# A two-block transformer kernel: the order of high and low weight products inside a half unit

## The chip, the cores and the metric

The kernel runs on one core of one Trainium2 chip. The metric is the device time of one execution, in microseconds. Before the change it is 2764.68 us, the median of three runs (2763.32 to 2768.03). Smaller is better.

## The reference

The program computes two transformer blocks on 256 tokens of width 2048, all in float32. What matters here is that nearly all of its work is products of activations with large weights:

```
first block:   h = rmsnorm(x);  proj = h @ w_in   (RG-LRU, rope attention with sinks, gates)
               x = x + rmsnorm(mix @ w_out)
               u = square(relu(rmsnorm(x) @ w_mlp_up));  x = x + rmsnorm(u @ w_mlp_down)
second block:  h = rmsnorm_2(x);  proj = h @ w_in   (dilated, block-sparse and compressed attention)
               x = x + concat(o_a, o_b, o_c) @ w_out
               a, g = split(conv3(rmsnorm_2(x) @ w_up));  x = x + (silu(g) * a) @ w_down
out = rmsnorm_2(x)
```

## The kernel before, in words

TensorE multiplies in fp32r, a format that keeps fewer bits than float32. To keep float32 accuracy, every operand is split in two: a high part, which is the value rounded to fp32r, and a low part, which is the value minus its high part. A product is then high weight times high activation, plus high weight times low activation, plus low weight times high activation.

**Tiling.** Activations are held with features on the partitions: a tile such as `h2` is 128 partitions x 16 chunks x (high, low) x 256 tokens. One output tile of 128 features x 256 tokens needs 16 chunks of 128 input features. The weights for it, 128 x 16 x 128 values, are a *unit* (1 MB; FD units have 11 chunks). The table `STREAM` lists 25 stages with their numbers of units, in the order in which they are used (X, RG, Q, Y, V, G, MR, MA, O, UP0, DN0, and so on to FD1). Each unit is worked off in two *half units* of 8 chunks (6 and 5 in FD).

**The weights' way.** SyncE loads a unit into `w_raw` (two buffers). ScalarE (line 1278, `half_hi`) copies a half unit to `w_hi`, rounding it, and raises `hi_ready`. VectorE (line 1972, `half_lo`) subtracts `w_hi` from `w_raw` into `w_lo` and raises `lo_ready`; only then may SyncE load the next unit into that `w_raw` buffer. There are four places for half units in `w2`. ScalarE overwrites a place when `half_done` shows that TensorE has finished the half unit that lay there.

**The products.** `half_unit` (line 626) issues a half unit on TensorE. In its wide form one matmul multiplies a chunk's high weights with the chunk's high and low activations side by side: 512 moving columns into one whole PSUM bank (line 634; "a high" below). A second matmul multiplies the low weights with the high activations: 256 moving columns, added to the bank's second half (line 638; "a low"). Each matmul is preceded by its own load of 128 weight columns. All highs of a half unit are issued first, behind a wait for `hi_ready`; then comes a wait for `lo_ready`, then all lows. The last low raises `half_done`. When a unit is finished, VectorE (line 1983) or ScalarE (line 1892) reads the two halves of the bank and adds them.

`half_unit` is called by `product` (line 744), `product2` (line 775, where two units add into one bank), `product_three` (line 717) and by the attention stages G and A2 themselves. Where its argument `ready` is given, each high also waits for its chunk of activations. The narrow form (`wide=False`) is used for the stages OC and OA alone.

Two other functions issue the same two kinds of matmul. `first_pair` (line 657) begins stage X with two units at a time: 16 highs, then 16 lows, then 16 pairs of one high and one low (lines 669 and 674), in which the accumulating bank alternates. `first_three` (line 696) begins UP0 and C2 with three units at a time, and issues a high and its low in pairs throughout (lines 712 and 714).

Of the kernel before, what the change touches and what calls it, by code (L numbers as in the profile page):

```python
# [25 lines left out]
P = 128  # L26
S = 256
# [104 lines left out]
def program(nc, dram):  # L132
    with ExitStack() as ctx:
# [120 lines left out]
        PS = ctx.enter_context(nc.psum_tensor("PS", [P, 8, 512], F32))  # L254

        def sem(name):
            return ctx.enter_context(nc.semaphore(name))
# [10 lines left out]
        lo_ready = sem("lo_ready")  # L268
        half_done = sem("half_done")
# [348 lines left out]
        def _(pe):  # L618
# [7 lines left out]
            def half_unit(u, s, hf, n, bank, rhs, k0, start, stop, ready=None, wide=True, slot=None, order=None):  # L626

                if wide:
                    w0, w1 = ((slot if slot is not None else w2[:, 2 * s + hf])[:, part, :] for part in range(2))
                    pe.wait_ge(hi_ready, 2 * u + hf + 1)  # L630
                    for k in range(n):
                        if ready:
                            pe.wait_ge(ready[0], ready[1] + k0 + k + 1)
                        pe.matmul(PS[:, bank, :], w0[:, k * P:(k + 1) * P],  # L634
                                  rhs[:, k0 + k].rearrange("p a b -> p (a b)"), start=start and k == 0, stop=False)
                    pe.wait_ge(lo_ready, 4 + 2 * u + hf + 1)
                    for k in range(n):
                        mm = pe.matmul(PS[:, bank, S:2 * S], w1[:, k * P:(k + 1) * P],  # L638
                                       rhs[:, k0 + k, 0, :], start=False, stop=stop and k == n - 1)
                    mm.then_inc(half_done, 1)  # L640
                else:
                    pe.wait_ge(lo_ready, 4 + 2 * u + hf + 1)
                    order = list(order or range(n))
                    for k in order:
                        if ready:
                            pe.wait_ge(ready[0], ready[1] + k0 + k + 1)
                        w0, w1 = (w[:, 2 * s + hf, k * P:(k + 1) * P] for w in (w_hi, w_lo))
                        r = rhs[:, k0 + k]
                        last = stop and k == order[-1]
                        acc = PS[:, bank, 0:S]  # L650
                        pe.matmul(acc, w0, r[:, 0, :], start=start and k == order[0], stop=False)  # L651
                        pe.matmul(acc, w0, r[:, 1, :], start=False, stop=False)  # L652
                        mm = pe.matmul(acc, w1, r[:, 0, :], start=False, stop=last)  # L653
                    if stop or len(order) == n:
                        mm.then_inc(half_done, 1)
# [61 lines left out]
            def product_three(name, n, rhs, ready, extra, banks, behind):  # L717

                u = U0[name]

                def unit(c, bank, evicted):
                    pe.wait_ge(acc_free, 2 + T0[name] + evicted)
                    half_unit(u + c, c % 2, 0, HALF, bank, rhs, 0, True, False)
                    half_unit(u + c, c % 2, 1, HALF, bank, rhs, HALF, False, True)

                first_three(name, rhs, ready, extra, banks)
                unit(3, banks[3], 0)
                unit(4, 0, 1)
                unit(5, 1, 2)
                done = 6  # L730
                for upto, then in behind:
                    for c in range(done, upto):
                        unit(c, c % 2, c - 1)
                    then()
                    done = upto
                if done == n:
                    return
                with pe.Fori(done // 2, n // 2) as i:
                    for s in range(2):
                        pe.wait_ge(acc_free, T0[name] + 2 * i + s + 1)  # L740
                        half_unit(u + 2 * i + s, s, 0, HALF, s, rhs, 0, True, False)
                        half_unit(u + 2 * i + s, s, 1, HALF, s, rhs, HALF, False, True)
# [117 lines left out]
            with pe.Fori(0, 2) as bh:  # L860
                pe.wait_ge(xr_lo, 8 * bh + 8)
                for hx in range(4):
                    s, hf = hx // 2, hx % 2
                    u = U0["RG"] + 2 * bh + s
                    pe.wait_ge(lo_ready, 4 + 2 * u + hf + 1)
                    pe.wait_ge(rg_evac, 4 * bh + hx + 1)
                    for b in range(2):
                        for m in range(2):
                            acc = PS[:, 2 + 2 * hf + b, m * S:(m + 1) * S]
                            for kk in range(2):  # L870
                                sub = (b * 2 + m) * 2 + kk
                                w0, w1 = (w[:, 2 * s + hf, sub * P:(sub + 1) * P] for w in (w_hi, w_lo))
# [3 lines left out]
                                mm = pe.matmul(acc, w1, r0, start=False, stop=kk == 1)  # L876
# [108 lines left out]
            for j in range(CMP_LEN):  # L985
                for br in range(2):
                    lo, up = HD * br, HD * br + HD
                    mm = pe.matmul(PS[:, 2 + br, 0:KV_C * N_CMP], cw1[lo:up, j, :],
                                   kpe[lo:up].rearrange("p v n j -> p (v n) j")[:, :, j],
                                   start=j == 0, stop=j == CMP_LEN - 1)  # L990
# [4 lines left out]
            for kv in range(KV_C):  # L995
                mm = pe.matmul(PS[0:N_CMP, 7, kv * HD:(kv + 1) * HD], hid[:, 1, kv * N_CMP:(kv + 1) * N_CMP],
                               cw2[:, 1, :], start=True, stop=True)
# [7 lines left out]
            def turn2(bank, e, slot):  # L1005
                for b in range(3):
                    mm = pe.transpose(PS[:, bank, b * P:(b + 1) * P], sb2[:, e, slot, b * P:(b + 1) * P], ident)  # L1007
                return mm
# [140 lines left out]
            for k in range(4):  # L1149
# [10 lines left out]
                for g in range(2):  # L1160
                    mm = turn2(5 + g, e, g)
# [46 lines left out]
            for h in range(NC_D // 2):  # L1208
# [5 lines left out]
                for n, (j, k) in enumerate(steps):  # L1214
# [4 lines left out]
                    w0, w1 = (w[:, h % 4, sub * P:(sub + 1) * P] for w in (w_hi, w_lo))  # L1219
                    pe.matmul(acc, w0, h_hi[:, 6 + k, :], start=k == 0, stop=False)  # L1220
                    pe.matmul(acc, w0, h_lo[:, 6 + k, :], start=False, stop=False)
                    mm = pe.matmul(acc, w1, h_hi[:, 6 + k, :], start=False, stop=k == SUB_B - 1)
# [1828 lines left out]
```

## Time and profile before

| what | value |
|---|---|
| median of 3 runs | 2764.68 us (2763.32 to 2768.03) |
| profiled execution, first to last instruction | 2763.6 us |
| TensorE matmul busy | 2724.2 us, 99%, 16376 matmuls |
| TensorE weight load busy | 2391.9 us, 87%, 16376 loads |
| VectorE busy | 1950.9 us, 71% |
| ScalarE busy | 1340.0 us, 48% |
| GpSimd busy | 110.2 us, 4% |
| HBM traffic over the span | 185 GB/s |

The profile lists no time of its own for the profiled execution beside this span; the span lies 1.1 us under the median of the runs. Matmuls overlap each other in the profile, since their ends are modelled: a high is listed with some 393 ns although the next one starts some 230 ns later. So what a matmul costs is read from the distance between starts and not from its duration. The timeline and the chain give starts to 0.01 us; a rate is read from a long run of them.

### The profile page before, as it was taken

How to read it: one execution, taken by the hardware profiler on the slowest of the kernel's cores; microseconds unless marked ns; L12 is line 12 of the kernel's file. 1: busy time of each engine (PE TensorE's matmuls, PEld its weight loads, DVE VectorE, ACT ScalarE, POOL GpSimd, SP SyncE). 2: the span in 40 equal slices, each digit the busy share in tenths (PEclk: the TensorE clock that was granted, in tenths of full speed). 3: DMA queues.
4: the chain of work that ended last, by engine and by line, in shares of the span. 5: the costliest groups of instructions: out<-in, count | busy, mean ns of one | idle time of the engine just before them, and what ended most of it. 6: DMA issues, size and time to landing. Idle time of an engine off the chain costs nothing.

```text
span 2763.6 us, 49219 instructions
## 1 busy us (share of the span) xinstructions
PE 2724.2 (99%) x16376; PEld 2391.9 (87%) x16376; DVE 1950.9 (71%) x3026; ACT 1340.0 (48%) x2132; POOL 110.2 (4%) x206
## 2 busy tenths in 40 slices
PE   8999999999999999999999999999999999999998
PEld 7888988888888888888888898898988888888887
DVE  8788777777767764456655765866798875688855
ACT  6755555554454443334444444644654444444443
POOL 0000000001010000000000000100000000000000
PEclk9999999999999999999999999999999999999999
DMA  6454544445563556656554554444555555555554
GB/s 215 174 178 172 200 153 150 150 171 183 182 210 142 196 192 216 206 204 213 216 197 183 183 185 161 148 169 150 180 178 186 188 180 188 191 191 186 182 168 166
DMA packets 83165, 503.24 MB, mean 182 GB/s; under 512 B 9674, under 2 KB 17914, under 8 KB 31504
## 3 DMA queue, kind: packets, MB, share of 16 engines
q1 hardware_dynamic: 79824, 490.77, 50.7%
q0 software_dynamic: 3120, 11.14, 1.2%
q8 instruction: 48, 0.79, 0.1%
q10 hardware_dynamic: 144, 0.30, 0.0%
q14 instruction: 29, 0.24, 0.0%
HBM read 500.02 MB, written 10.55 MB: 185 GB/s over the span
## 4 chain that ended last, share of the span: by engine, by line
PE 93%; DVE 4%; ACT 1%; issue 1%; DMA 1%; DVEq 0%; ACTq 0%; SPq 0%
PE PS L634 53%; PE PS L638 27%; PE PS L816 1%; PE PS L817 1%; PE PS L818 1%; PE PS L651 1%; PE PS L652 1%; PE PS L653 1%; PE PS L712 1%; PE PS L1007 1%; DVE w L1972 1%; ACT w L1278 0%; DMA w_raw<-in_w_C 0%; PE PS L913 0%; DMA w_raw<-in_w_DN 0%
## 5 line engine op out<-in xcount | busy, mean ns | idle before, releaser
L1972 DVE TENSOR_TENSOR w<-w_raw,w 128x1024 fp32r<-128x1024 f32 (+2 forms) x916 | 1040.0, 1168 | 337.0 <-ACT w L1278 334.5
L1278 ACT ACTIVATE w<-w_raw 128x1024 fp32r<-128x1024 f32 (+2 forms) x916 | 893.4, 1007 | 342.8 <-PE PS L638 192.6
L634 PE MATMUL PS<-h,w 128*128 128x512 f32 x2976 | 756.1, 396 | 0.8 <-ACT w L1278 0.8
L634 PEld LDWEIGHTS PS<-h,w 128*128 128x128 f32 x2976 | 535.4, 189 | 112.6 <-issue 14.2
L634 PE MATMUL PS<-u,w 128*128 128x512 f32 x1680 | 429.5, 394 | 3.7 <-ACT w L1278 3.7
L638 PEld LDWEIGHTS PS<-h,w 128*128 128x128 f32 x2976 | 405.8, 190 | 29.6
L638 PE MATMUL PS<-h,w 128*128 128x256 f32 x2976 | 414.4, 282 | 0.0
L634 PE MATMUL PS<-f,w 128*128 128x512 f32 x1408 | 352.7, 392 | 0.0
L634 PEld LDWEIGHTS PS<-u,w 128*128 128x128 f32 x1680 | 300.2, 189 | 55.1 <-ACT w L1278 4.1
L634 PEld LDWEIGHTS PS<-f,w 128*128 128x128 f32 x1408 | 253.3, 189 | 45.3
L638 PEld LDWEIGHTS PS<-u,w 128*128 128x128 f32 x1680 | 235.1, 191 | 20.6
L638 PE MATMUL PS<-u,w 128*128 128x256 f32 x1680 | 241.1, 283 | 0.0
L638 PEld LDWEIGHTS PS<-f,w 128*128 128x128 f32 x1408 | 192.1, 190 | 13.7
L638 PE MATMUL PS<-f,w 128*128 128x256 f32 x1408 | 196.3, 282 | 0.0
L1892 ACT ACTIVATE low<-PS 128x256 f32<-128x256 f32 x88 | 33.9, 385 | 205.5 <-PE PS L638 205.5
L1619 ACT ACTIVATE u<-tmp 128x256 f32 (+1 forms) x64 | 26.7, 417 | 194.9 <-DVE tmp L2507 194.9
L634 PE MATMUL PS<-d,w 128*128 128x512 f32 x464 | 116.4, 393 | 0.5 <-ACT w L1278 0.5
L1983 DVE TENSOR_REDUCE tmp<-PS 128x256 f32<-128x512 f32 x99 | 68.3, 690 | 48.3 <-PE PS L638 45.1
L634 PEld LDWEIGHTS PS<-d,w 128*128 128x128 f32 x464 | 83.4, 189 | 15.8 <-issue 0.8
L816 PE MATMUL PS<-w,h 128*128 128x256 f32 x256 | 74.2, 290 | 0.8 <-DVE tmp L1983 0.8
L817 PE MATMUL PS<-w,h 128*128 128x256 f32 x256 | 73.5, 287 | 0.0
L818 PE MATMUL PS<-w,h 128*128 128x256 f32 x256 | 73.4, 287 | 0.0
(394 smaller groups left out, 2739.6 us busy)
## 6 DMA issues: line engine op xcount, KB each, us to landing
w_raw<-in_w_FU SPq DMA_DIRECT2D x88, 1024.0 KB, 4.8
w_raw<-in_w_UP SPq DMA_DIRECT2D x64, 1024.0 KB, 4.8
w_raw<-in_w_DN SPq DMA_DIRECT2D x64, 1024.0 KB, 4.9
w_raw<-in_w_FD SPq DMA_DIRECT2D x64, 704.0 KB, 4.1
w_raw<-in_w_G SPq DMA_DIRECT2D x32, 1024.0 KB, 4.8
w_raw<-in_w_Q SPq DMA_DIRECT2D x18, 1024.0 KB, 4.9
w_raw<-in_w_X SPq DMA_DIRECT2D x16, 1024.0 KB, 4.9
w_raw<-in_w_Y SPq DMA_DIRECT2D x16, 1024.0 KB, 4.8
```

The costliest lines, as they stand in the source:

```text
L634: pe.matmul(PS[:, bank, :], w0[:, k * P:(k + 1) * P], rhs[:, k0 + k].rearrange("p a b -> p (a b)"), start=start and k == 0, stop=False)
L638: mm = pe.matmul(PS[:, bank, S:2 * S], w1[:, k * P:(k + 1) * P], rhs[:, k0 + k, 0, :], start=False, stop=stop and k == n - 1)
L651: pe.matmul(acc, w0, r[:, 0, :], start=start and k == order[0], stop=False)
L652: pe.matmul(acc, w0, r[:, 1, :], start=False, stop=False)
L653: mm = pe.matmul(acc, w1, r[:, 0, :], start=False, stop=last)
L816: pe.matmul(acc, a0, w0, start=c == 0, stop=False)
L817: pe.matmul(acc, a0, w1, start=False, stop=False)
L818: mm = pe.matmul(acc, a1, w0, start=False, stop=c == NC_D - 1)
L1278: act.activation(w_hi[:, 2 * s + hf, 0:n * P], w_raw[:, s, off * P:(off + n) * P], ACT.Copy)\
L1892: act.activation(low[:, s, :], PS[:, s, S:2 * S], ACT.Copy).then_inc(low_ready, 1)
L1972: tt(w_lo[:, slot, 0:n * P], w_raw[:, s, off * P:(off + n) * P], w_hi[:, slot, 0:n * P].bitcast(F32), ALU.subtract).then_inc(lo_ready, 1)
L1983: return dve.tensor_reduce(out, PS[:, s, :].rearrange("p (a b) -> p b a", a=2), AX.X, ALU.add)
```

## The change

In the wide form of `half_unit`, the low of chunk k - 1 is issued right behind the high of chunk k. The wait for `lo_ready` moves from behind the last high to behind the second one. The matmuls, their operands, their number and the accumulation into the bank are the same; the first high still opens the accumulation, and the last low still closes it and raises `half_done`. `first_pair`, `first_three` and the narrow form are as they were. In the changed file the high is line 639 and the low is line 632.

```diff
 
                 if wide:
                     w0, w1 = ((slot if slot is not None else w2[:, 2 * s + hf])[:, part, :] for part in range(2))
+
+                    def low_part(k):
+                        return pe.matmul(PS[:, bank, S:2 * S], w1[:, k * P:(k + 1) * P],
+                                         rhs[:, k0 + k, 0, :], start=False, stop=stop and k == n - 1)
+
                     pe.wait_ge(hi_ready, 2 * u + hf + 1)
                     for k in range(n):
                         if ready:
                             pe.wait_ge(ready[0], ready[1] + k0 + k + 1)
                         pe.matmul(PS[:, bank, :], w0[:, k * P:(k + 1) * P],
                                   rhs[:, k0 + k].rearrange("p a b -> p (a b)"), start=start and k == 0, stop=False)
-                    pe.wait_ge(lo_ready, 4 + 2 * u + hf + 1)
-                    for k in range(n):
-                        mm = pe.matmul(PS[:, bank, S:2 * S], w1[:, k * P:(k + 1) * P],
-                                       rhs[:, k0 + k, 0, :], start=False, stop=stop and k == n - 1)
-                    mm.then_inc(half_done, 1)
+                        if k == 1:
+                            pe.wait_ge(lo_ready, 4 + 2 * u + hf + 1)
+                        if k:
+                            low_part(k - 1)
+                    low_part(n - 1).then_inc(half_done, 1)
                 else:
```

How the rows move on TensorE. First place: the last half unit of the last loop (stage FD, 5 chunks); `u_59` is the activations, `w_50` the buffer of split weights, and a REGISTER_ALU row works out the number that the next wait compares with. Before:

```order
L630 REGISTER_ALU
L634 MATMUL PS<-u_59,w_50 128x512 [waits hi_ready]
L634 MATMUL PS<-u_59,w_50 128x512 x4
L636 REGISTER_ALU
L638 MATMUL PS<-u_59,w_50 128x256 [waits lo_ready]
L638 MATMUL PS<-u_59,w_50 128x256 x4
L789 REGISTER_ALU
L789 COMPARE_AND_BRANCH
```

With the change:

```order
L635 REGISTER_ALU
L639 MATMUL PS<-u_59,w_50 128x512 [waits hi_ready]
L639 MATMUL PS<-u_59,w_50 128x512
L642 REGISTER_ALU
L632 MATMUL PS<-u_59,w_50 128x256 [waits lo_ready]
L639 MATMUL PS<-u_59,w_50 128x512
L632 MATMUL PS<-u_59,w_50 128x256
L639 MATMUL PS<-u_59,w_50 128x512
L632 MATMUL PS<-u_59,w_50 128x256
L639 MATMUL PS<-u_59,w_50 128x512
L632 MATMUL PS<-u_59,w_50 128x256 x2
L794 REGISTER_ALU
```

Two highs now stand ahead of the first low and its wait for `lo_ready`, where five did; then highs and lows alternate, and two lows end the half unit.

Second place: the first half unit of stage FD1 (6 chunks), where each high waits for its activations. Before, with the start of the half unit behind it:

```order
L634 MATMUL PS<-u_59,w_50 128x512 [waits u_ready,hi_ready,acc_free]
L634 MATMUL PS<-u_59,w_50 128x512 [waits u_ready] x5
L638 MATMUL PS<-u_59,w_50 128x256 [waits lo_ready]
L638 MATMUL PS<-u_59,w_50 128x256 x5
L634 MATMUL PS<-u_59,w_50 128x512 [waits u_ready,hi_ready]
L634 MATMUL PS<-u_59,w_50 128x512 [waits u_ready] x4
```

With the change:

```order
L639 MATMUL PS<-u_59,w_50 128x512 [waits u_ready,hi_ready,acc_free]
L639 MATMUL PS<-u_59,w_50 128x512 [waits u_ready]
L632 MATMUL PS<-u_59,w_50 128x256 [waits lo_ready]
L639 MATMUL PS<-u_59,w_50 128x512 [waits u_ready]
L632 MATMUL PS<-u_59,w_50 128x256
L639 MATMUL PS<-u_59,w_50 128x512 [waits u_ready]
L632 MATMUL PS<-u_59,w_50 128x256
L639 MATMUL PS<-u_59,w_50 128x512 [waits u_ready]
L632 MATMUL PS<-u_59,w_50 128x256
L639 MATMUL PS<-u_59,w_50 128x512 [waits u_ready]
L632 MATMUL PS<-u_59,w_50 128x256 x2
L639 MATMUL PS<-u_59,w_50 128x512 [waits u_ready,hi_ready]
```

The waits for activations stay with their highs; the wait for `lo_ready` now stands behind one of them and ahead of the other four.

## Rows read from the trace of the kernel before

**Rows 1.** The page: span, engines, TensorE's granted clock, and the chain's shares by line.
```profile
span 2763.6 us, 49219 instructions
PE 2724.2 (99%) x16376; PEld 2391.9 (87%) x16376; DVE 1950.9 (71%) x3026; ACT 1340.0 (48%) x2132; POOL 110.2 (4%) x206
...
PEclk9999999999999999999999999999999999999999
...
PE PS L634 53%; PE PS L638 27%; PE PS L816 1%; PE PS L817 1%; PE PS L818 1%; PE PS L651 1%; PE PS L652 1%; PE PS L653 1%; PE PS L712 1%; PE PS L1007 1%; DVE w L1972 1%; ACT w L1278 0%; DMA w_raw<-in_w_C 0%; PE PS L913 0%; DMA w_raw<-in_w_DN 0%
```

**Rows 2.** One line's view, L634 matmuls: duration ns min/median/max, first and last start.
```profile
L634 PE MATMUL PS<-h,w x2976: 387/393/582, 26.0 to 1818.3; 128*128 128x512 f32 x199
L634 PE MATMUL PS<-u,w x1680: 389/393/628, 1024.7 to 2749.9; 128*128 128x512 f32 x187
L634 PE MATMUL PS<-f,w x1408: 389/391/582, 2005.1 to 2621.9; 128*128 128x512 f32 x176
L634 PE MATMUL PS<-d,w x464: 389/393/499, 567.7 to 829.9; 128*128 128x512 f32 x155
L634 PE MATMUL PS<-d,w3u x48: 389/391/397, 797.6 to 835.5; 128*128 128x512 f32 x48
L634 PE MATMUL PS<-u,w3c x48: 389/391/398, 1521.9 to 1559.9; 128*128 128x512 f32 x48
```

**Rows 3.** The chain of waits, 1060 to 1155 us: start us, us, what.
```profile
1061.19 1.84 PE PS L634 x8
...
1153.37 1.84 PE PS L634 x8
```

**Rows 4.** The timeline of PE, 14 to 26 us: start, length, line, count.
```profile
14.06 3.79 PE L669 MATMUL PS<-h,w 128*128 128x512 f32 x16
17.68 2.08 PE L674 MATMUL PS<-h,w 128*128 128x256 f32 x16
19.60 0.40 PE L669 MATMUL PS<-h,w 128*128 128x512 f32 x1
...
19.95 0.40 PE L669 MATMUL PS<-h,w 128*128 128x512 f32 x1
...
20.31 0.40 PE L669 MATMUL PS<-h,w 128*128 128x512 f32 x1
...
24.90 0.40 PE L669 MATMUL PS<-h,w 128*128 128x512 f32 x1
```

**Rows 5.** The timeline of PE, 849 to 862 us (product UP0).
```profile
849.81 0.40 PE L712 MATMUL PS<-h,w4u 128*128 128x512 f32 x1
...
861.47 0.40 PE L712 MATMUL PS<-h,w4u 128*128 128x512 f32 x1
```

**Rows 6.** The timeline of PE, 1575 to 1587 us (product C2).
```profile
1575.42 0.39 PE L712 MATMUL PS<-h,w4c 128*128 128x512 f32 x1
...
1586.86 0.39 PE L712 MATMUL PS<-h,w4c 128*128 128x512 f32 x1
```

**Rows 7.** The waits of PE: engine, line, waited for: us in total, times, longest.
```profile
PE PS L634 <- ACT w L1278: 4.9, 5, 2.5
```

**Rows 8.** The timeline of DVE and PE at three half units.
```profile
2018.26 2.35 DVE L1972 TENSOR_TENSOR w<-w_raw,w 128x1024 fp32r<-128x1024 f32 x2
...
2017.92 2.00 PE L634 MATMUL PS<-f,w 128*128 128x512 f32 x8
...
907.08 2.36 DVE L1972 TENSOR_TENSOR w<-w_raw,w 128x1024 fp32r<-128x1024 f32 x2
...
906.88 2.08 PE L634 MATMUL PS<-h,w 128*128 128x512 f32 x8 [0.21 <-ACT w L1278]
...
138.58 2.36 DVE L1972 TENSOR_TENSOR w<-w_raw,w 128x1024 fp32r<-128x1024 f32 x2 [1.09 <-ACT w L1278]
...
138.69 2.06 PE L634 MATMUL PS<-h,w 128*128 128x512 f32 x8 [0.57 <-ACT w L1278]
```

## The prediction

> **What bounds the kernel now.** I read the page first. TensorE is busy 99% of a span of 2763.6 us, and the chain that ended last runs through its highs (line 634, 53%) and its lows (line 638, 27%) [rows 1]. No other line has more than 1%. The granted clock is 9 tenths or more in all 40 slices, so practically the whole span is at the upper of TensorE's two levels, 2.4 GHz. At that clock 512 columns take 213.3 ns and 256 columns take 106.7 ns. So the question is how far apart matmuls start, and whether a wait opens a hole between them. The other engines matter only through `hi_ready` and `lo_ready`.
>
> Second, the view of line 634 gives the number of highs: 2976 + 1680 + 1408 + 464 + 48 + 48 = 6624 [rows 2]. FD has 64 units of 11 chunks, thus 704 of these highs, in 128 half units of 6 or 5. The other 5920 make 740 half units of 8. Each high has one low.
>
> Third, the distance between starts. In the chain, 33 half units of 8 chunks take 1153.37 - 1061.19 = 92.18 us [rows 3], that is 2.793 us each, or 349.2 ns for a high and its low. The start of stage X shows long runs of one kind. Sixteen highs take 17.68 - 14.06 = 3.62 us, 226 ns each; sixteen lows take 19.60 - 17.68 = 1.92 us, 120 ns each [rows 4]. Both are 13 ns above their columns' time. I call 226.7 + 120 = 346.7 ns the clean pair. Eight clean pairs are 2.773 us, so **a half unit loses 20 ns somewhere**, and it has just one turn from lows back to highs.
>
> **What alternation costs.** The trace of before has it already, in three stretches without a hole:
> - in `first_pair`, right behind the run of lows, 15 pairs take 24.90 - 19.60 = 5.30 us, 353.3 ns each [rows 4];
> - in `first_three` of UP0, 33 pairs take 861.47 - 849.81 = 11.66 us, 353.3 ns each [rows 5];
> - in `first_three` of C2, 33 pairs take 1586.86 - 1575.42 = 11.44 us, 346.7 ns each [rows 6].
>
> So alternation runs at one of two rates. Either it is clean, or it loses 6.7 ns at every turn from a low to a high. The same loop shows both, and I do not know what selects one. The two stretches of `first_three` began behind a hole; the stretch of `first_pair` began without one, behind a run of lows, and its first pairs are no cheaper or dearer than the later ones: 19.95 - 19.60 = 0.35 and 20.31 - 19.95 = 0.36 us [rows 4]. The changed half units begin behind two lows, and mostly without a hole. That is nearest to the stretch of `first_pair`, so I take its rate.
>
> **The sum.** Nothing is added or removed: as many matmuls, loads, columns and waits. What moves:
> 1. *Turns in 8-chunk half units.* Before, one turn at 20 ns. Changed: six turns from one low to one high, and one turn from two lows to two highs. At 6.7 ns for all seven this is 47 ns, 27 ns more. 740 x 27 ns = **+20 us**. It all lies on the path. The bounds: all seven clean, 740 x -20 ns = -15 us; and six at 6.7 ns with the double turn still at 20, 740 x +40 ns = +30 us.
> 2. *FD.* Here it is on average 3.5 single turns and a double one, 30 ns against 20. 128 x 10 ns = **+1 us** (bounds -3 and +3).
> 3. *The wait for `lo_ready`.* The first low used to come 8 highs (1.84 us) behind the half unit's start, and now 2 highs (0.46 us) behind it. Most half units have their low weights long before. They are late where TensorE has just waited for ScalarE's copy, since VectorE's subtraction of 2.36 / 2 = 1.18 us begins only then. Before, such waits came 5 times [rows 7]. At 138.69 us VectorE starts at 138.58 and is done at 139.76; the first low would start near 139.2, 0.6 us too early. At 906.88 VectorE starts only at 907.08, is done at 908.26, and the low would start at 907.4: 0.8 us [rows 8]. Four at 0.6 and one at 0.8 make 3.2 us. A further place is a busy VectorE: at 2017.92 it is done with the half at 2018.26 + 1.18 = 2019.44, against 2018.38, 1.1 us late [rows 8]. Behind the waiting low stand six highs that could have run; ScalarE and VectorE wait for nothing in it. 3.2 + 1.1 gives **+4 us**, between 1 us, if later waits for `hi_ready` shrink in return, and 6 us, with two more such places that I did not find.
> 4. *Everything else*: nothing. The last low of a half unit ends where it did, and with it `half_done`, ScalarE's next copy and the reading of the bank. Where highs wait for activations a low could now fill a hole, but the waits of PE name nothing but ScalarE's copy in front of line 634 [rows 7]. SyncE's loads follow `lo_ready`, which VectorE raises at the same time as before unless `half_done` moves.
>
> The sum is +20 + 1 + 4 = +25 us on the span of 2763.6, so 2789; the median lies 1.1 us above the span, which gives **2790 us**, +0.9%.
>
> **A rule weighed.** The rows show 120 ns between lows and 226 between highs, 13 ns above the columns in both [rows 4]. The Trainium skill (TensorE: Matmul & The Clock Gate, section "Back-to-back issue gap") gives a warm gap of N / 2.4 + 2.5 ns, whatever stood before. By that an order of the same matmuls is free, and the change is worth nothing but its waits; the trace differs both in the size (13 and not 2.5 ns) and in that a turn costs something. The same page's section on LDWEIGHTS gives 107 ns for 128 columns, which would just hide behind a low's columns and easily behind a high's. No row here separates the load's share: in the clean stretch alternation is as fast as the two runs, and not faster.
>
> **The rivals.**
> - *A, the forecast: alternation loses at every turn.* For it: two of the three stretches, and the one that starts most like a half unit. Against it: rows 6. 2782 to 2801 us, by the bounds of terms 1 and 3.
> - *B, faster: alternation runs clean and the 20 ns of each half unit go away.* The mechanism is that the loss of before belongs to the turn from a long run of lows to a long run of highs, of which there is none left. For it: 33 pairs at 346.7 ns [rows 6]. The sum is -15 - 3 + 4 = -14 us, 2751. It decides as soon as a turn costs less than 20 / 7 = 2.9 ns on average. Against it: the clean stretch began behind a hole, and each half unit here starts anew behind two lows.
> - *C, no change: single turns are clean, but the double turn at the end of each half unit keeps its 20 ns.* Then only the waits are left, +4 us, 2769. A mixture, in which some stages run at one rate and some at the other, comes out here too: half and half is (25 - 14) / 2 = +5 us. The skill's rule above gives the same time.
> - *D, the waits are dearer.* If VectorE is late for many more half units than the ones I saw, each costs 0.6 to 1.1 us. The page's 71% for VectorE speaks against it, and ten more places at 0.6 to 1.1 us would add 6 to 11 us to A: about 2799.
> - That the change does not do what it says can be excluded by the order of the rows.
>
> **How the numbers follow.** A measurement of this kernel can tell about 0.2% from no change, that is 5.5 us: 2759.2 to 2770.2. I give A 0.50 and D 0.05, both slower; C 0.19, of which 0.02 fall on the slower side; B 0.26. So faster 0.26, same 0.17, slower 0.57. The range for eight in ten reaches from B's value to A's upper part: 2750 to 2801. A alone would be 2782 to 2801.
>
> **What would show it.** In the chain of the changed kernel, 33 half units near 1061 us take 33 x 2.820 = 93.1 us under A, 91.5 under B and 92.2 under C. The timeline shows pairs of 353 ns under A, at steps of 0.35, 0.36, 0.35, and of 347 under B. For term 3, the waits of PE have a new row, line 632 waiting for line 1972 of VectorE, with 4 to 8 waits and 3 to 5 us in total. I am wrong if the 8-chunk half unit takes 2.78 us or less, or if that row has more than 8 us.

## The result, and the profile after

The changed kernel takes 2790.3 us, the median of four runs (2787.82 to 2790.78), against 2764.62 us (median of four runs, 2763.32 to 2768.03) before. The ratio is 1.0087, with a 95% interval from 1.0075 to 1.0100: it is slower, by 0.9%. The forecast was 2790.

The page of the changed kernel first, in the lines that answer to [rows 1]. Line 639 is now the high and line 632 the low.

```profile
span 2789.0 us, 49219 instructions
...
PE 2749.0 (99%) x16376; PEld 2389.7 (86%) x16376; DVE 1951.8 (70%) x3026; ACT 1340.5 (48%) x2132; POOL 110.3 (4%) x206
...
PEclk9999999999999999999999999999999999999999
...
PE PS L639 53%; PE PS L632 27%; PE PS L821 1%; PE PS L822 1%; PE PS L823 1%; PE PS L656 1%; DVE w L1977 1%; PE PS L657 1%; PE PS L658 1%; PE PS L717 1%; PE PS L1012 1%; PE PS L993 0%; DMA w_raw<-in_w_C 0%; PE PS L918 0%; DMA w_raw<-in_w_DN 
```

The span is 25.4 us longer, the clock row has a 9 in each slice as before, and the chain still runs through highs and lows in the same shares. So no new thing bounds the kernel. The same work goes by more slowly, or with more holes.

A slice is some 70 us long, though, and hides one difference. In the compression stage (128 small matmuls of 45 columns, line 988 before and line 993 in the changed file) the granted clock fell to the lower level, 1.2 GHz, in both executions, but it stayed there for 6.8 us before and for 13.6 us in the changed kernel. The matmuls first (start, length, line, count), before and changed:

```profile
1651.01 8.12 PE L988 MATMUL PS<-kpe,cw 64*128 64x45 f32 x128
```

```profile
1665.05 11.09 PE L993 MATMUL PS<-kpe,cw 64*128 64x45 f32 x128
```

Then the stages view (window, its length, busy us and number of matmuls started, clock, DMA share, GB/s), before and changed:

```profile
1657.40:1664.20 6.80, 6.80 (x42) 0.50 0.05 10
```

```profile
1668.20:1681.80 13.60, 13.60 (x103) 0.50 0.04 11
```

The change does not touch these matmuls. Counted from the same matmul to the same matmul in both traces, this stretch is 3.2 us longer in the changed kernel. So about 22 of the 25.4 us are left for the order and the wait. The other stretches at the lower level are as long in both traces, to about 1 us.

The chain of waits of the changed kernel (start us, us, what) answers to [rows 3]. It shows the two highs with which every half unit opens. Between the first and the last row below lie 34 half units of 8 chunks:

```profile
1061.87 0.47 PE PS L639 x2
...
1157.75 0.47 PE PS L639 x2
```

(1157.75 - 1061.87) / 34 = 2.820 us a half unit, where it was 2.793: 27 ns more. The timeline of TensorE shows the inside of one (start, length, line, count), which answers to [rows 4] and [rows 5]:

```profile
1061.71 0.63 PE L639 MATMUL PS<-u,w 128*128 128x512 f32 x2
1062.18 0.28 PE L632 MATMUL PS<-u,w 128*128 128x256 f32 x1
1062.29 0.39 PE L639 MATMUL PS<-u,w 128*128 128x512 f32 x1
1062.52 0.28 PE L632 MATMUL PS<-u,w 128*128 128x256 f32 x1
1062.63 0.40 PE L639 MATMUL PS<-u,w 128*128 128x512 f32 x1
...
1062.98 0.40 PE L639 MATMUL PS<-u,w 128*128 128x512 f32 x1
...
1063.35 0.40 PE L639 MATMUL PS<-u,w 128*128 128x512 f32 x1
...
1063.69 0.40 PE L639 MATMUL PS<-u,w 128*128 128x512 f32 x1
```

Two highs open it, and then highs and lows alternate. From the high at 1062.63 to the next at 1062.98 it is 0.35 us, then 0.37 and 0.34: the scattered steps of the lossy rate, three pairs in 1.06 us, as in [rows 5]. The first pair, from 1062.29 to 1062.63, is shorter.

The stages view, for the highs alone (window, its length, busy us and number of highs started, clock, DMA share, GB/s), gives the rate over 500 us without a hole. The changed kernel, and then the one before:

```profile
1000.00:1500.00 500.00, 486.89 (x1420) 1.00 0.58 204
```

```profile
1000.00:1500.00 500.00, 358.56 (x1433) 1.00 0.58 205
```

500 / 1420 = 352.1 ns for a high and its low, against 500 / 1433 = 348.9 ns. The clock is 1.00 in both and the DMA share is 0.58 in both, so neither explains the difference here.

In the stage FD the half units are shorter. The timeline of the changed kernel, at the starts of a half unit of 6, one of 5, and the next; then the same of before (6 highs from 2273.20, 5 from 2271.45):

```profile
2284.28 0.62 PE L639 MATMUL PS<-u,w 128*128 128x512 f32 x2
...
2286.39 0.64 PE L639 MATMUL PS<-u,w 128*128 128x512 f32 x2
...
2288.14 0.62 PE L639 MATMUL PS<-u,w 128*128 128x512 f32 x2
```

```profile
2271.45 1.32 PE L634 MATMUL PS<-u,w 128*128 128x512 f32 x5
...
2273.20 1.55 PE L634 MATMUL PS<-u,w 128*128 128x512 f32 x6
...
2275.30 1.09 PE L634 MATMUL PS<-u,w 128*128 128x512 f32 x4
```

The half unit of 6 takes 2.11 us and was 2.10; that of 5 takes 1.75 and was 1.75. Here the change costs next to nothing.

Last, the waits of TensorE (engine, line, waited for: us in total, times, longest) answer to [rows 7]:

```profile
PE PS L639 <- ACT w L1283: 4.2, 3, 2.5
...
PE PS L632 <- DVE w L1977: 2.8, 7, 0.7
```

There is a new row, in which the low waits for VectorE's subtraction: 7 times, 2.8 us. The waits for ScalarE went down from 4.9 to 4.2 us. One of the new waits, on VectorE and then on TensorE, is the place at 138.69 us of [rows 8]:

```profile
139.53 2.36 DVE L1977 TENSOR_TENSOR w<-w_raw,w 128x1024 fp32r<-128x1024 f32 x2 [1.09 <-ACT w L1283]
```

```profile
139.65 0.70 PE L639 MATMUL PS<-h,w 128*128 128x512 f32 x2 [0.52 <-ACT w L1283]
140.81 0.39 PE L632 MATMUL PS<-h,w 128*128 128x256 f32 x1 [0.47 <-DVE w L1977]
```

TensorE waits for the copy, starts two highs, and finds the low weights not there: they come at 139.53 + 1.18 = 140.71. Before, six more highs ran in that time. Yet the end result is not 0.47 us lost. The matmul behind this half unit (line 885 before, line 890 changed) needs something else of VectorE, and before it was TensorE's wait for that which came last. Before, then changed:

```profile
142.40 0.70 PE L885 MATMUL PS<-tmp,const 128*128 128x256 f32 x2 [0.69 <-DVE tmp L2252]
```

```profile
143.35 0.70 PE L890 MATMUL PS<-tmp,const 128*128 128x256 f32 x2
```

The 0.69 us of idle time are gone in the changed kernel, so this one late low costs nothing on the path.

### The profile page after: what moved, and what is told of

Same layout as the page of the kernel before. It is cut to its first block, busy times and chain, and to the rows that moved or that the text cites. A ratio compares the mean times of both kernels' runs of the same rounds, so it can differ in the third digit from the quotient of the medians.

```text
span 2789.0 us, 49219 instructions
## 1 busy us (share of the span) xinstructions
PE 2749.0 (99%) x16376; PEld 2389.7 (86%) x16376; DVE 1951.8 (70%) x3026; ACT 1340.5 (48%) x2132; POOL 110.3 (4%) x206
## 4 chain that ended last, share of the span: by engine, by line
PE 93%; DVE 4%; ACT 1%; DMA 1%; issue 1%; DVEq 0%; ACTq 0%; SPq 0%
PE PS L639 53%; PE PS L632 27%; PE PS L821 1%; PE PS L822 1%; PE PS L823 1%; PE PS L656 1%; DVE w L1977 1%; PE PS L657 1%; PE PS L658 1%; PE PS L717 1%; PE PS L1012 1%; PE PS L993 0%; DMA w_raw<-in_w_C 0%; PE PS L918 0%; DMA w_raw<-in_w_DN 0%
## 5 line engine op out<-in xcount | busy, mean ns | idle before, releaser
L639 PE MATMUL PS<-h,w 128*128 128x512 f32 x2976 | 1031.3, 401 | 0.5 <-ACT w L1283 0.5
L632 PE MATMUL PS<-h,w 128*128 128x256 f32 x2976 | 775.0, 281 | 1.5 <-DVE w L1977 1.5
L639 PEld LDWEIGHTS PS<-h,w 128*128 128x128 f32 x2976 | 534.6, 188 | 117.5 <-issue 13.8
L632 PEld LDWEIGHTS PS<-h,w 128*128 128x128 f32 x2976 | 561.8, 189 | 37.9 <-DVE w L1977 3.2
L639 PE MATMUL PS<-u,w 128*128 128x512 f32 x1680 | 574.0, 398 | 3.7 <-ACT w L1283 3.7
L639 PE MATMUL PS<-f,w 128*128 128x512 f32 x1408 | 483.5, 398 | 0.0
L632 PE MATMUL PS<-u,w 128*128 128x256 f32 x1680 | 431.2, 281 | 0.3 <-DVE w L1977 0.3
L632 PE MATMUL PS<-f,w 128*128 128x256 f32 x1408 | 366.7, 281 | 0.7 <-DVE w L1977 0.7
L632 PE MATMUL PS<-d,w 128*128 128x256 f32 x464 | 120.9, 281 | 0.4 <-DVE w L1977 0.4
L639 PEld LDWEIGHTS PS<-d,w 128*128 128x128 f32 x464 | 83.3, 188 | 16.0 <-issue 0.2
L632 PEld LDWEIGHTS PS<-d,w 128*128 128x128 f32 x464 | 87.6, 189 | 6.3 <-DVE w L1977 0.8
L821 PE MATMUL PS<-w,h 128*128 128x256 f32 x256 | 74.3, 290 | 0.8 <-DVE tmp L1988 0.8
```

The costliest lines, as they stand in the source:

```text
L632: return pe.matmul(PS[:, bank, S:2 * S], w1[:, k * P:(k + 1) * P], rhs[:, k0 + k, 0, :], start=False, stop=stop and k == n - 1)
L639: pe.matmul(PS[:, bank, :], w0[:, k * P:(k + 1) * P], rhs[:, k0 + k].rearrange("p a b -> p (a b)"), start=start and k == 0, stop=False)
L821: pe.matmul(acc, a0, w0, start=c == 0, stop=False)
```

## The experiments

The theory at this point: TensorE loses time where it turns from a low to a high, and the loss for each turn depends on what stands around it; 20 us of the change are that, and 4 us the moved wait. (This leaves out the stretch at the lower clock.) The rivals are that the wait carries most of it, and that the 20 ns lost in each half unit of before belong to the half unit and not to the turn. Each kernel was timed beside the kernel before on the same chip; that one took 2765.61 us beside mirror, early_wait, blocks1 and blocks2, and 2764.84 us beside blocks4 and wide_low, and each ratio is to the time beside it. In the diffs, which are excerpts, `high(k)` and `low_part(k)` stand for the two matmuls of chunk k, and the wait for activations is left out. A summary, with the half unit of 8 chunks in a stretch without holes:

| kernel | order of a half unit | half unit, us | median, us | ratio to before, 95% |
|---|---|---|---|---|
| before | 8 highs, 8 lows | 2.793 | 2764.62 | 1 |
| the change | 2 highs, then in turn, 2 lows | 2.820 | 2790.30 | 1.0087 [1.0075, 1.0100] |
| early_wait | 8 highs, 8 lows, early wait | 2.793 | 2771.08 | 1.0022 [1.0012, 1.0031] |
| blocks1 | strictly in turn | 2.77 or 2.83 | 2783.24 | 1.0071 [1.0054, 1.0088] |
| blocks2 | in twos | 2.787 | 2765.29 | 1.0000 [0.9990, 1.0009] |
| blocks4 | in fours | 2.800 or 2.807 | 2776.60 | 1.0043 [1.0027, 1.0060] |
| mirror | 8 highs, 16 lows, 8 highs, for a unit | 2.783 | 2757.98 | 0.9975 [0.9965, 0.9985] |

### mirror: fewer turns

In the second half unit of a unit the lows come first, so that highs meet highs at the border of two units:

```diff
+flip = hf == 1 and not ready
 pe.wait_ge(hi_ready, 2 * u + hf + 1)
-for k in range(n):
-    high(k)
+if not flip:
+    for k in range(n):
+        high(k)
 pe.wait_ge(lo_ready, 4 + 2 * u + hf + 1)
 for k in range(n):
     low_part(k)
+if flip:
+    for k in range(n):
+        high(k)
```

Expected: 

> Before's order in the first half unit of a unit (8 highs, 8 lows); in the second half unit the lows come first, then the highs (except where highs wait for activations). A unit then has one turn from lows to highs in place of two. Theory (the 20 ns of a half unit belong to the turn from a run of lows to a run of highs): the first half unit and the second together take 5.566 us in place of 5.586, 20 ns less in each of about 420 units, so 8 us less, 2756 us. Rival (the 20 ns belong to the half unit itself, to its waits or its last low): nothing changes, 2764 us. Second rival (the early wait for lo_ready in the second half unit costs more than the turn gives): above 2766 us.

Measured: 2757.98 us (10 runs, 2756.32 to 2761.06) against 2765.61 beside it, a ratio of 0.9975 with an interval from 0.9965 to 0.9985. The timeline of TensorE, at three rows and again 14 units later (highs in line 633, lows in line 637):

```profile
1064.11 3.82 PE L633 MATMUL PS<-u,w 128*128 128x512 f32 x16
1067.77 2.08 PE L637 MATMUL PS<-u,w 128*128 128x256 f32 x16
1069.68 3.82 PE L633 MATMUL PS<-u,w 128*128 128x512 f32 x16
...
1142.04 3.82 PE L633 MATMUL PS<-u,w 128*128 128x512 f32 x16
```

(1142.04 - 1064.11) / 14 = 5.566 us a unit, where before has 2 x 2.793 = 5.586. 20 ns less in each of at most 370 units of two 8-chunk half units would be 7.4 us; the ratio of 0.9975 is 6.9 us. So the loss belongs to the turn, and not to the half unit or its waits: half as many turns, half the loss, and a turn from 16 lows to 16 highs costs no more than one from 8 to 8. The second rival falls as well. The waits of TensorE have no row for a low that waits for its weights; this is the one row of its main products:

```profile
PE PS L633 <- ACT w L1289: 5.5, 6, 2.6
```

This version beats both kernels.

### early_wait: the wait alone

```diff
 for k in range(n):
+    if k == 2:
+        pe.wait_ge(lo_ready, 4 + 2 * u + hf + 1)
     high(k)
-pe.wait_ge(lo_ready, 4 + 2 * u + hf + 1)
 for k in range(n):
     low_part(k)
```

Expected: 

> Before's order, 8 highs and then 8 lows, with the wait for lo_ready alone moved to behind the second high, where the change has it. Theory (turns cost 20 us and more, waits about 4): half units stay at 2.793 us and the time rises by 3 to 6 us, to 2768 to 2771 us. Rival (the moved wait carries most of the change's 26 us): 2780 us or more.

Measured: 2771.08 us, a ratio of 1.0022 (1.0012 to 1.0031). The page's first line, the timeline (high 636, low 639) and the waits:

```profile
span 2768.1 us, 49241 instructions
```

```profile
1060.36 2.00 PE L636 MATMUL PS<-u,w 128*128 128x512 f32 x8
1062.20 1.11 PE L639 MATMUL PS<-u,w 128*128 128x256 f32 x8
1063.15 1.55 PE L636 MATMUL PS<-u,w 128*128 128x512 f32 x6
```

```profile
PE PS L636 <- ACT w L1279: 4.7, 4, 2.5
...
PE PS L636 <- DVE w L1973: 3.2, 8, 0.7
```

The half unit is 2.79 us as before, and the span is 2768.1 - 2763.6 = 4.5 us longer, with the clock at the lower level as long as before. The waits for VectorE are 3.2 us, 8 of them. By the medians it is 5.5 us, and the ratio's interval reaches from 3 to 9 us. So the moved wait costs some 5 us by itself, and most of the change is the order. The rival that the wait carries most of it falls.

### blocks1: strictly in turn, and two rates from one code

```diff
-for k in range(n): high(k)
-pe.wait_ge(lo_ready, ...)
-for k in range(n): low_part(k)
+for k in range(n):
+    high(k)
+    if k == 0: pe.wait_ge(lo_ready, ...)
+    low_part(k)
```

Expected: 

> Strict pairs: each low right behind its own high, so that a half unit of 8 has 8 single turns and no double one. Theory (6.7 ns at every turn of an alternation): 8 x 6.7 = 53 ns lost in place of 20, 33 ns x 740 = 24 us, 2 us in FD, 5 to 6 us of waits, as the first low comes behind one high: 2795 to 2797 us, half unit 2.826 us. Rival (the double turn at the end of the change's half units is what loses, single turns are clean): half unit 2.773 us and 2764 - 15 + 6 = 2755 us.

Measured: 2783.24 us (four runs, 2777.84 to 2787.34), ratio 1.0071 (1.0054 to 1.0088), faster than the theory said and slower than the rival. Neither had it right, and the stages view of the highs shows why:

```profile
260.00:330.00 70.00, 70.00 (x203) 1.00 0.55 194
...
1000.00:1500.00 500.00, 500.00 (x1417) 1.00 0.57 203
2060.00:2250.00 190.00, 190.00 (x549) 1.00 0.54 189
```

70 / 203 = 345 and 190 / 549 = 346 ns a pair at the beginning and towards the end, the clean rate of [rows 6]; but 500 / 1417 = 353 ns in the long stretch, the lossy rate of [rows 5]. So alternation has just the two rates that the trace of before showed, and keeps one for hundreds of microseconds. What picks it? The same kernel was profiled in one more execution.

Expected: 

> The same kernel as blocks1, strict pairs. There, whole stretches ran at 346.7 ns a pair and others at 353.3, and the rate changed only behind a hole (lossy from 928 to 1619 us, clean from 2034 to 2266 us). If the rate is picked afresh at a hole, by timing, some stretches stand at the other rate in this execution and the time differs by several us; the half unit is again 2.773 or 2.82 to 2.83 us, nothing between. If addresses pick it, every stretch has the rate that it had, and the span is again 2776 us.

```profile
260.00:330.00 70.00, 70.00 (x200) 1.00 0.55 194
...
1000.00:1500.00 500.00, 500.00 (x1444) 1.00 0.58 206
2060.00:2250.00 190.00, 190.00 (x539) 1.00 0.53 186
```

In all three windows the rate has changed over: 350, 346 and 353 ns. (The first window is short, so that its count is good to some 0.5% only.) The code, the data and the addresses are the same. So addresses don't pick the rate. It is picked anew where the stream of matmuls has been interrupted, and in the long stretches it is then kept until the next hole: in the two traces, 1822 pairs without a hole run at 353.3 ns in the one and at 346.7 ns in the other. (In the last 115 us, in FD, both rates occur within one stretch.) The span is 2767.4 where it was 2776.1, but not all of these 8.7 us are the rate: the first execution also spent 10 us more at the lower clock, which by an estimate from the granted clock, half of that time, is 5 us. What in the timing of a hole decides it stays open.

### blocks2 and blocks4: how much a turn costs between short runs

```diff
+for j in range(0, n, b):            # b = 2, b = 4
+    for k in range(j, min(j + b, n)): high(k)
+    if j == 0: pe.wait_ge(lo_ready, ...)
+    for k in range(j, min(j + b, n)): low_part(k)
```

Expected of twos: 

> Two highs, two lows, four times over: four double turns in a half unit of 8. If every turn costs 6.7 ns, 27 ns are lost in place of 20: +7 ns, and with the waits 2773 us. If a turn between runs costs 20 ns whatever the runs' length, 80 ns are lost: +60 ns x 740 = 44 us, 2813 us. The half unit is 2.800 us by the first and 2.853 us by the second.

Measured: 2765.29 us, ratio 1.0000 (0.9990 to 1.0009). The timeline, with two highs at a time (line 633), and the stages view:

```profile
1060.17 0.63 PE L633 MATMUL PS<-u,w 128*128 128x512 f32 x2
...
1060.87 0.63 PE L633 MATMUL PS<-u,w 128*128 128x512 f32 x2
...
1062.96 0.63 PE L633 MATMUL PS<-u,w 128*128 128x512 f32 x2
```

```profile
1000.00:1500.00 500.00, 450.77 (x1436) 1.00 0.58 205
```

From 1060.17 to 1062.96 it is four such blocks, 2.79 us; 500 / 1436 = 348.2 ns a pair, so 8 x 348.2 = 2.786 us. Eight clean pairs are 2.773, so four turns lose 13 ns, 3 ns each. That is less than either theory said: the turns give back 7 ns x 740 = 5 us, and the early wait of about 4 us eats it.

Expected of fours: 

> Four highs, four lows, twice over: two turns in a half unit of 8, with the wait for lo_ready behind the fourth high. Blocks of 2 lost 13.5 ns in four turns, runs of 8 lose 20 ns in one. If a turn costs more the longer the runs beside it are, two turns cost between 2 x 3.4 and 2 x 20 = 7 to 40 ns; by the step between, some 12 ns each: half unit 2.797 us, +3 us for the turns and +1 to +2 for the waits, 2768 to 2771 us. If a turn from lows always costs 20 ns once the highs come four in a row, 2.813 us and 2780 us.

Measured: 2776.60 us, ratio 1.0043 (1.0027 to 1.0060). The stages view, in two stretches:

```profile
590.00:690.00 100.00, 77.64 (x285) 1.00 0.52 181
1000.00:1500.00 500.00, 387.70 (x1429) 1.00 0.58 206
```

100 / 285 = 350.9 ns and 500 / 1429 = 349.9 ns a pair, thus 2.807 and 2.799 us a half unit: two turns lose 34 ns in one stretch and 26 in the other, 17 or 13 ns each. The half unit is as the step between said, or a little above, but the median is 5 us above the 2768 to 2771 expected. The profiled execution was the fastest of the four: 2772.36 us at a mean granted clock of 0.997, where the others have 0.996 (2775.43 us) and 0.995 (2777.76 and 2777.92 us). So most of the spread, and of the 5 us, goes with the clock. The two stretches show that fours, too, run at more than one rate.

### wide_low: all matmuls of one width

```diff
-pe.matmul(PS[:, bank, S:2 * S], w1[...], rhs[:, k0 + k, 0, :], ...)
+pe.matmul(PS[:, bank, :], w1[...], rhs[:, k0 + k].rearrange("p a b -> p (a b)"), ...)
```

Expected: 

> The change's order, but each low multiplies all 512 columns (it adds the product of low weight and low activation, which the kernel leaves out), so that all matmuls are of one width. Theory (the turn between widths is what costs): every start is 226.7 ns behind the last one, a half unit of 8 takes 16 x 226.7 = 3627 ns, with nothing lost. Rival (changing between the two weight parts, or between two chunks of activations, costs): 47 ns more, 3674 ns, with distances that scatter by 6 ns and more. Time about 2790 + 6624 x 0.107 = 3495 us.

Measured: 3451.68 us (one execution). The time was expected 43 us too high: that sum started from the change's time and left in the losses of its turns (740 x 47 ns = 35 us), which had to go away. The other 8 us are not assigned. The timeline, at the two highs that open three half units (line 639):

```profile
1401.33 0.62 PE L639 MATMUL PS<-u,w 128*128 128x512 f32 x2
...
1404.96 0.61 PE L639 MATMUL PS<-u,w 128*128 128x512 f32 x2
...
1408.58 0.62 PE L639 MATMUL PS<-u,w 128*128 128x512 f32 x2
```

(1408.58 - 1401.33) / 2 = 3.625 us, for 16 matmuls 226.6 ns each. The change's order, with another weight part and another chunk of activations at every step, runs without any loss as soon as all matmuls have 512 columns. So it is neither the change of weight part nor that of chunk that costs. With the width, wide_low also changes the part of the PSUM bank that a low writes (the whole in place of its second half) and the activations that it reads. That the width itself is what counts, and not the part of the bank, is the simplest reading and was not tested apart.

## Why the prediction was right, point by point

- **The bound.** That the distance of starts and the waits set the time held for 22 of the 25.4 us. The sum had no term for the clock: in the compression stage it stood at the lower level for 13.6 us in place of 6.8, which is 3.2 us. Whether the changed order had a part in this, or only the moment of the execution, is not known; of the four timed executions of the changed kernel three had a mean clock of 0.995 (2790.3 to 2790.8 us) and one 0.997 (2787.82 us), and the kernel before shows 0.995 to 0.997 as well.
- **Term 1, turns in half units of 8.** Predicted +27 ns a half unit and +20 us. Measured in the long stretch: 2.820 - 2.793 = 27 ns. Summed over all 740 half units of the two traces it is 18.6 us, 25 ns each; 643 of them gain 24 to 30 ns, and those beside holes less. The choice between the two rates of alternation was the step on which the sign hung, and it was taken from the stretch most like the changed one. The reason given, that the half unit starts behind lows and without a hole, is borne out in part: in the changed trace 635 of the 740 half units take 2.815 to 2.824 us and five less than 2.81, so it has the lossy rate wherever no hole falls into them, while strict pairs take either rate and keep it. That the two runs of two at a half unit's border are what ties the change to the lossy rate was not tested.
- **Term 2, FD.** Predicted +10 ns on average and +1 us. The half unit of 6 has 7 ns more and that of 5 none (starts in the traces, to 1 ns); 128 half units make 0.4 us. The rule of 6.7 ns for each turn does not hold in short half units.
- **Term 3, the wait.** Predicted +4 us. In the changed kernel's own trace, the eleven half units that differ most from before, those with holes, make 3.0 us together beyond their turns; early_wait has +4.5 us in its span. The new row has the 7 waits that were forecast as 4 to 8, but 2.8 us where 3 to 5 were forecast. Of the single places, 0.6 us was given for 138.69; the wait is 0.47 us there, and costs nothing, since a later wait shrinks by as much.
- **The sum.** The forecast 20 + 1 + 4 = 25 came out as 18.6 + 0.4 + 3.0 = 22.0 us in the traces, 3.2 us are the clock, and 0.2 us are not assigned. So each term was right in kind and 0.6 to 1.4 us too large. That 2790 was hit exactly is luck: the clock, which no term had, made up for it.
- **The uniform cost of a turn.** This step was too simple, though it gave nearly the right sum. Blocks of two lose 3 ns a turn, blocks of four 13 or 17, runs of eight and of sixteen 20, single turns 0 or 6.7.
- **Rival B**, that alternation runs clean, describes a rate that exists: strict pairs have it in part of their stretches, and in that part gain 20 ns a half unit on before. The changed order does not get it.
- **Rival C**, no change, is where the blocks of two came out. **Rival D**, many more late subtractions, falls with the 7 waits.
- **The rule weighed.** The Trainium skill (TensorE: Matmul & The Clock Gate, section "Back-to-back issue gap") gives one gap for a width, with no term for what stood before. The runs contradict that for mixed widths: a half unit of the same matmuls took 2.77 to 2.83 us, by the order and the stretch. They also show 226.7 ns for 512 columns where that rule gives 215.8. What the prediction left out is that the same section calls this the gap of a matmul by itself, and gives 131 ns at 512 columns for a stream in which each matmul has its weight load, as here. No run shows that either: over hundreds of microseconds it is 226.7 ns.

## What to carry to other kernels

When TensorE is busy all the time, the order of equal work still counts for a per cent: where matmuls of different widths must mix, count the turns from narrow to wide and make them few, for instance by mirroring every second group, which added no wait for low weights here. Do not alternate widths because one stretch of a trace shows it running clean; the same code can fall into either of two rates at each interruption, so read long stretches and more than one execution. Compare the granted clock stage by stage too, since a page of 40 slices hid 3 us of it here. And before moving a wait forward, list the places where the producer has only just been released: most of them pay, although nearly all half units have their low weights in time, and one pays nothing where a later wait takes it up.

## What the runs showed of the hardware that was not expected

- A turn from 256-column to 512-column matmuls costs 20 ns between runs of 5, 6, 8 or 16, 13 or 17 ns between fours, 3 ns between twos; between single ones it is either nothing or 6.7 ns. The 20 ns do not fall at the turn alone. In the trace of before, the highs behind a turn start 233.3, 235.8, 228.3, 232.5 and 230.8 ns apart, and only then 226.7; the first two lows behind a high give 7.5 ns back (113.3 and 119.2 in place of 120).
- Which of the two rates single turns get is not a property of the code. In two executions of one kernel the same 500 us ran at 353 ns a pair (1417 highs) and at 346 ns (1444 highs), at a granted clock of 1.00 both times.
- With all matmuls at 512 columns nothing is lost, though weight parts and chunks alternate as in the change: 226.6 ns each.
- The granted clock differs between executions of one kernel, and the time goes with it: of 10 runs of mirror, three at 0.997 took 2756.3 to 2756.7 us, five at 0.996 took 2757.7 to 2759.3, and two at 0.995 took 2760.2 and 2761.1.
